# Three normalizers moved ahead of two state updates in the last stage of a GLA/HGRN2 decoder layer

## The reference

```
proj = rms_norm(x) @ w_in, split into GLA (4 heads) and HGRN2 (8 heads) parts and two gates
o_gla, s_gla_new = chunked_gated_linear(q, k, v, log_a, s_gla)      # S_t = diag(a_t) S_(t-1) + k_t^T v_t
o_hg,  s_hg_new  = chunked_gated_linear(q2, k2, v2, lf, s_hg)       # o_t = q_t S_t
merged = sigmoid(ga) * head_norm_gate(o_gla) + sigmoid(gb) * head_norm_gate(o_hg)
h  = x + rms_norm(merged @ w_out)
x' = h + rms_norm((silu(a) * u) @ w_ffn_out),   [a, u] = rms_norm(h) @ w_ffn_in
```

## Time and profile before

| | |
|---|---|
| median of three runs | 1074.19 us |
| the profiled execution's own time | 1074.19 us |
| its span | 1072.4 us |
| PE busy | 1052.7 us, 98% |
| DVE busy | 673.9 us, 63% |
| ACT busy | 478.4 us, 45% |
| POOL busy | 69.6 us, 6% |
| mean granted TensorE clock | 0.998 of full |

### The profile page before, as it was taken

The page is one execution under the profiler, slowest core; times in us unless marked ns, Lnnn a source line. Parts: engine busy times, 40 slices in busy tenths (PEclk is TensorE's granted clock), DMA queues, the critical chain, the costliest instruction groups (busy, mean ns, idle before and its releaser), DMA issues.

```text
span 1072.4 us, 25184 instructions
## 1 busy us (share of the span) xinstructions
PE 1052.7 (98%) x11040; PEld 992.5 (93%) x11040; DVE 673.9 (63%) x978; ACT 478.4 (45%) x760; POOL 69.6 (6%) x87
## 2 busy tenths in 40 slices
PE   7999999999999999999999999899999999999997
PEld 5999999999999999999999877799999999988886
DVE  6265625666426756356755489998888888744544
ACT  6433344632436433446325537644444444533532
POOL 5100003100004000030000021000000000000000
PEclk9999999999999999999999999999999999999999
DMA  6522223622217322146222292033424333422212
GB/s 192 162 76 77 64 70 100 197 62 68 76 48 216 90 70 80 51 117 180 61 80 70 66 299 59 15 104 84 114 79 113 85 87 92 138 79 79 79 59 88
DMA packets 138717, 105.30 MB, mean 98 GB/s; under 512 B 4017, under 2 KB 123825, under 8 KB 138609
## 3 DMA queue, kind: packets, MB, share of 16 engines
q1 hardware_dynamic: 133744, 85.88, 28.2%
q0 software_dynamic: 4864, 17.83, 5.6%
HBM read 91.89 MB, written 11.80 MB: 97 GB/s over the span
## 4 chain that ended last, share of the span: by engine, by line
PE 89%; DVE 5%; ACT 2%; DVEq 1%; DMA 1%; ACTq 1%; issue 1%; POOL 0%; SPq 0%; POOLq 0%
PE ps L255 43%; PE ps L1807 21%; PE ps L1831 13%; PE ps L1029 2%; PE ps L1060 1%; PE ps L1050 1%; PE ps L1006 1%; PE ps L1062 1%; PE ps L1067 1%; DMA w_raw_t<-in_w_out_dram 1%; PE ps L1043 1%; PE ps L1098 1%; PE ps L1025 1%; PE ps L1087 0%; PE ps L1013 0%
## 5 line engine op out<-in xcount | busy, mean ns | idle before, releaser
L255 PE MATMUL ps<-x_hi,w_lo_t 128*128 128x288 f32 x1152 | 251.7, 300 | 0.0
L255 PE MATMUL ps<-x_hi,w_hi_t 128*128 128x288 f32 x1152 | 246.3, 295 | 0.0
L255 PE MATMUL ps<-x_lo,w_hi_t 128*128 128x288 f32 x1152 | 246.2, 295 | 0.0
L241 ACT ACTIVATE w_hi_t<-w_raw_t 128x1024 fp32r<-128x1024 f32 x73 | 77.2, 1058 | 308.1 <-PE ps L255 307.7
L245 DVE TENSOR_TENSOR w_lo_t<-w_raw_t,w_hi_t 128x1024 fp32r<-128x1024 f32 x73 | 89.2, 1222 | 169.2 <-ACT w_hi_t L241 168.8
L255 PEld LDWEIGHTS ps<-x_hi,w_lo_t 128*128 128x128 f32 x1152 | 184.1, 189 | 4.3 <-issue 2.5
L255 PEld LDWEIGHTS ps<-x_hi,w_hi_t 128*128 128x128 f32 x1152 | 185.3, 188 | 0.0
L255 PEld LDWEIGHTS ps<-x_lo,w_hi_t 128*128 128x128 f32 x1152 | 185.2, 188 | 0.0
L1807 PE MATMUL ps<-x_hi,w_lo_t 128*128 128x288 f32 x264 | 78.4, 297 | 3.6 <-DVE work L1623 2.4
L1807 PE MATMUL ps<-x_hi,w_hi_t 128*128 128x288 f32 x264 | 78.2, 296 | 0.0
L1807 PE MATMUL ps<-x_lo,w_hi_t 128*128 128x288 f32 x264 | 78.2, 296 | 0.0
(11 more groups left out here) (302 smaller groups left out, 2104.9 us busy)
## 6 DMA issues: line engine op xcount, KB each, us to landing
w_raw_t<-in_w_in_dram SPq DMA_DIRECT2D x73, 512.0 KB, 3.8
merged<-in_w_ffn_in_dram SPq DMA_DIRECT2D x22, 512.0 KB, 5.2
w_raw_t<-in_w_ffn_in_dram SPq DMA_DIRECT2D x22, 512.0 KB, 4.6
w_raw_t<-in_w_ffn_out_dram SPq DMA_DIRECT2D x22, 512.0 KB, 3.7
h_t<-in_x_prompt_dram SPq DMA_DIRECT2D x8, 512.0 KB, 5.6
h_t<-in_state_gla_dram POOLq DMA_DIRECT2D x4, 1024.0 KB, 6.4
h_t<-in_state_hgrn_dram POOLq DMA_DIRECT2D x8, 512.0 KB, 8.0
out_dram<-h_t POOLq DMA_DIRECT2D x4, 1024.0 KB, 6.2
```

Source lines behind the costliest of these rows:

```text
L241: nc.scalar.activation(w_hi_t[:, u % NSPL, 0:nk, :], w_raw_t[:, u % NRAW, 0:nk, :], ACT.Copy).then_inc(w_hi, 1)
L255: m = nc.tensor.matmul(out[:, q, :], w[:, u % NSPL, k, :], x(k, q), start=first and i == 0, stop=last and i == len(todo) - 1)
```

## The change

- `LAST`: norm1 and norm2 move from the third group to the second, and ss2 and ss3 from the second to the third, behind norm0. The last numbers become ss0 105, ss1 106, norm1 107, norm2 108, norm0 109, ss2 110, ss3 111.
- ACT: the roots of norm1 and norm2 come ahead of W4's hi, and W5's hi comes last, behind the last two copies of `merged`.
- DVE: both gate products come before W3's lo. The scaling by norm1 and norm2 follows, then W4's lo, the scaling by norm0, both additions and both splits of `merged`. Only then come the state updates ss2 and ss3, and then W5's lo.
- SP: the wait for the last column of `merged` ahead of the load of `g_pre` is removed.

```
-LAST = {0: ["ss0", "ss1"], 1: ["ss2", "ss3"], 2: ["norm1", "norm2", "norm0"]}
+LAST = {0: ["ss0", "ss1"], 1: ["norm1", "norm2"], 2: ["norm0", "ss2", "ss3"]}
...
         out_hi(act, UB + 3)
+        norm(G - 1, (1, 2))
         out_hi(act, UB + 4)
-        out_hi(act, UB + 5)
-        norm(G - 1, (1, 2))
         norm(G - 1, (0,))
         for k in range(KT - 2, KT):
             act.wait_ge(merged_s, G + 1 + k - (KT - 2))
             early_hi(k)
+        out_hi(act, UB + 5)
...
         sample_states(G - 1, 1)
-        out_lo(dve, UB + 3)
         gated(G - 1, 0)
         gated(G - 1, 2)
-        sample_states(G - 1, 2)
-        sample_states(G - 1, 3)
-        out_lo(dve, UB + 4)
-        out_lo(dve, UB + 5)
+        out_lo(dve, UB + 3)
         dve.wait_ge(rst, (G - 1) * 3 + 2)
         dve.tensor_tensor(O[:, 2:4, :], O[:, 2:4, :], rs_two(G - 1), ALU.mult)
+        out_lo(dve, UB + 4)
         dve.wait_ge(rst, (G - 1) * 3 + 3)
         for i in range(2):
             dve.tensor_tensor(O[:, i, :], O[:, i, :], rs(G - 1, 0), ALU.mult)
-            if i == 1:
-                early_lo(KT - 2)
             dve.drain()
             dve.tensor_tensor(merged[:, KT - 2 + i, :], O[:, i, :], O[:, 2 + i, :], ALU.add).then_inc(merged_s, 1)
+        early_lo(KT - 2)
         early_lo(KT - 1)
+        sample_states(G - 1, 2)
+        sample_states(G - 1, 3)
+        out_lo(dve, UB + 5)
...
-        sp.wait_ge(merged_s, G + 2)
         sp.dma_start(g_pre, norm_ffn_pre.partition_broadcast(P).rearrange("p o d -> p (o d)")).then_inc(g_pre_in, 16)
```

## The result

The changed kernel takes 1082.99 us (median of four runs, 1082.35 to 1083.51) against 1074.16 us before on the same chip (1073.88 to 1075.56): a ratio of 1.0074, 95% interval 1.006 to 1.0088. It is 8.8 us slower by the medians, and 8.0 us (6.4 to 9.5) by the ratio. Forecast were 1081.9 us and a range of 1079.6 to 1084.2. Its profiled execution took 1080.87 us with a span of 1079.1 us. That execution and four more (1080.96, 1081.74, 1081.90 and 1082.37 us) are not among the four runs; the median of all nine is 1082.35 us.

The account below looks back on a forecast made before the run. PE was taken as the bound, with DVE, ACT and the DMAs just keeping up. To 1074.19 us it added 6.1 us of delay and 1.6 us of clock, giving 1081.9 us, range 1079.6 to 1084.2.

Parts of the forecast that it names:

- The two new waits: On PE: about 0.9 us before ss2 for ACT's logarithm of norm0, 6.4 us before the sample tile for DVE's update.
- Nothing else becomes late: After the sample tile's start: W5's lo hidden by 0.8 us, no wait for W7's lo, x loads in time.
- The step that called SP's removed wait worthless: SP's queue: removing the wait costs and gains nothing, since W5's lo, which W7's load awaits, is behind those additions anyway.
- DVE's chain behind: Hidden state's chain after W7: DVE 5.8 us and PE 6.4 us later, alternating over four tiles, taken as 6.1 us.
- The clock: Behind PE's new wait: granted clock falls to half level for about 3.4 us, costing 1.6 us.
- The rival of a longer fall: Behind PE's new wait: two half-clock stretches, 3.2 us instead of 1.6, giving 1083.5 us; chance 0.10.
- The held clock: Behind PE's new wait: clock granted at full level, only the 6.1 us delay, giving 1080.3 us; chance 0.13.
- taking up of the delay later: Behind W7: DVE comes out 2 us better and the fall at 679.6 doesn't recur, about 1078.5 us; chance 0.07.
- The late fall of the clock: Half clock from 679.6 to 683.0 us in the kernel before; its absence was counted as 1.5 us won.
- The loads: Stores and five x loads take 3 us over their longest rows, adding 1 to 2 us, 1084 us; chance 0.04.
- covered the bank wait: At the sample tile: PE doesn't wait for ss2, so the kernel is faster, 1071.9 us; chance 0.04.

Follow-up runs that it names:

- The first experiment: Changed kernel with state updates ss2, ss3 and W5's lo put back ahead of the scaling by norm0 on DVE, W5's hi moved on ACT; 1077.99 us, ratio 1.0029.
- wait filled: Changed kernel in which PE adds W2's product for token tile 0 four more times (24 matmuls) before waiting for ss2; 1079.57 us, ratio 1.0049.
- SP's wait kept: Changed kernel with SP's wait for the last column of merged kept ahead of the load of g_pre; 1082.54 us, ratio 1.0074.
- W5's lo ahead: Changed kernel with W5's lo on DVE ahead of the state updates ss2 and ss3; 1083.62 us, ratio 1.0084.
- W3 in the wait: Changed kernel in which PE does W3 of the four prompt tiles (24 matmuls) before waiting for ss2's read; 1082.98 us, ratio 1.0079.
- W3 in the wait, copies on ACT: Changed kernel with W3 of the prompt tiles done in PE's wait and the four FFN copies made by ACT instead of POOL; 1079.44 us, ratio 1.0041.
- changed, copies on ACT: Changed kernel with the four FFN copies made by ACT instead of POOL; 1082.69 us, ratio 1.0068.

## Why the prediction was right

**The two new waits.** Expected 0.9 us before ss2 and 6.4 us before the sample tile, released by ACT's logarithm and by DVE's update. The trace has 0.92 and 6.21 us with those releasers. The first experiment changed the second wait to the size that the theory gave, 2.25 us. Shown.

**Nothing else becomes late.** W5's lo ended at 636.7 and PE wanted it at 638.8; no wait for W7's lo appeared; x was loaded without anything waiting for it. The step that called SP's removed wait worthless holds (ratio 1.0074 with it and without it).

**DVE's chain behind.** I had taken a lasting delay of 6.1 us. With the clock held it measured 5.3 us. In that trace the first token tile is taken at 655.00, 4.8 us later than before, where I had 5.8. These traces start some 0.2 us earlier throughout, so it is really 5.0. The missing 0.8 us are three small terms. W2 started 1.72 us behind the two norms' start (616.24 to 617.96), not 2.10. From the sample tile to W7 PE took 19.59 us (633.08 to 652.67), not the 19.8 that the prediction has (633.7 to 653.5). And DVE took the tile 2.33 us behind W7's start, not 2.5.

**The clock.** This term of the sum was mis-sized: 1.6 us predicted, about 3.0 us measured (1082.54 less 1079.57, two kernels on one chip; 8.8 less 5.3 would be 3.5, from two chips). The rows locate it. I take PE's stretch from a state step ahead of the change to its first wait for an FFN weight; in the kernel before it goes from 609.78 to 674.84, 65.06 us.

```profile
609.78 1.15 PE L1098 MATMUL ps<-v_t,T 32*128 32x256 f32 x16
```

| kernel | PE's stretch, us | longer by | median less that of its kernel before |
|---|---|---|---|
| states back ahead | 610.38 to 678.62 | 3.2 | 3.7 |
| wait filled | 609.57 to 680.22 | 5.6 | 5.3 |
| changed | 609.58 to 681.69 | 7.1 | 8.8 |
| SP's wait kept | 610.18 to 683.44 | 8.2 | 8.3 |
| W5's lo ahead | 609.29 to 683.84 | 9.5 | 9.3 |
| W3 in the wait | 609.93 to 683.55 | 8.6 | 8.6 |
| W3 in the wait, copies on ACT | 610.75 to 680.76 | 5.0 | 4.4 |
| changed, copies on ACT | 609.97 to 683.26 | 8.2 | 7.7 |

But for the changed kernel, whose trace is one of its quick executions, the last two columns agree within 0.6 us: the whole cost lies in this stretch. The low clock takes 1.5 us of it in the changed kernel's trace and 2.6 us with SP's wait kept. It lasted 3.3 us into the work in the first, as the prediction had it (3.4), but 5.2 to 5.8 us in the three other traces with a wait over 6 us and nothing put into it. So the single stretch that I priced is the mild case here. What decides between the two isn't shown. The fall in the earlier trace rows, from which I took the price, cost nothing itself. The Trainium skill's rule ("TensorE: Matmul & The Clock Gate", Terms), throttled time times one half, gives as an estimate 1.6 us for 3.3 us of slow work and 2.9 us for 5.7; the traces agree with 1.5 and 2.6. The rule was right, and my estimate of the throttled time was too short. The rival of a longer fall (1083.5 us) is closer than the forecast (1081.9) to the median of the four runs, 1082.99; the forecast is the closer one to that of all nine, 1082.35.

**Luck in the sum.** The delay was put 0.8 us too high and the clock 1.4 us too low, and the two errors partly cancel. The forecast is right in its mechanism and sign; that it came within 1.1 us owes something to luck.

**The other rivals.** The held clock (1080.3 us) is refuted for this kernel, whose clock fell; where it was held, in the filled wait, the time was 1079.6 us. No taking up of the delay later was seen. The late fall of the clock didn't recur in the changed kernel's trace, but that saved nothing: the 1.5 us that the prediction counted for it in two of its rivals were never a cost. The loads were in time (longest landing 8.9 us), and nothing covered the bank wait.

## What to carry to other kernels

In an in-order queue, moving critical-looking work ahead also moves something back: ask who waits for the thing moved back, here PE, for a pair of banks read only by the state updates. The normalizers that were brought forward had been in time already. Where TensorE is the bound, price an idle stretch of several us at more than its length (here 5.3 us of delay and 3.0 us of clock behind a wait of 6.2 us), and look for work that can fill it, even if it doesn't shorten the chain. The work must fill it, though: W3 cut the wait to 3.4 us, opened another of 2.5 us, and won nothing.

## What the runs showed of the hardware that I had not expected

Two programs that differ only in a wait on SP that is always met, with the same 6.21 us wait on PE, came back to 2.4 GHz after 3.3 us of dense matmuls in one execution and after 5.7 us in the other; this makes 1.1 us between them. An added 5.6 us of matmuls, put into that wait, kept the clock at full level and took 3.0 us off the kernel. Behind a wait of 2.5 us (in the kernel with W3 in the wait), and behind one of 0.92 and one of 2.25 us (states back ahead), the clock fell as well; behind 0.92 and 0.53 us in the filled kernel it didn't. Behind the waits of 1.15 and 1.50 us it fell in the trace of the kernel before and not in that of the changed kernel, where the same waits lie at 681.7 and 685.0. In the kernel before, that fall of 3.4 us cost nothing, since PE would have stood for 1.5 us at full clock. And DVE's subtraction with 128x1024 elements took 2.0 us beside POOL's copy and 1.22 us without it.
